# A gated scan in log levels: score levels with two heads per product, the projection's units spread anew, and decayed keys' exponents by eight ScalarE activations

## The reference, cut to what matters

```python
q = jax.nn.silu(q)
f = lbh + (1.0 - lbh) * jax.nn.sigmoid(fpre)
k = 1.0 - f
logf = jnp.log(f)
...
b = jnp.cumsum(lfc, axis=2)
inter = jnp.einsum('bhtd,bhde->bhte', qc * jnp.exp(b), S)
diff = b[:, :, :, None, :] - b[:, :, None, :, :]
decay = jnp.exp(jnp.where(mask, diff, -jnp.inf))
A = jnp.einsum('bhtsd,bhsd->bhts', qc[:, :, :, None, :] * decay, kc)
intra = jnp.einsum('bhts,bhse->bhte', A, vc)
b_last = b[:, :, -1:, :]
S_new = jnp.exp(b_last[:, :, 0, :])[..., None] * S + jnp.einsum(
    'bhsd,bhse->bhde', kc * jnp.exp(b_last - b), vc)
```

## Time and profile before

| | |
|---|---|
| median of 3 runs | 3231.85 us (3229.95 to 3232.8) |
| the profiled execution | 3230.88 us, its span 3229.1 us |
| TensorE busy | 2908.6 us, 90% of the span |
| TensorE's weight loads | 2611.5 us, 81% |
| VectorE busy | 1680.7 us, 52% |
| ScalarE busy | 687.4 us, 21% |
| GpSimd busy | 1098.1 us, 34% |
| mean granted clock of TensorE | 0.949 of full speed |

### The profile page before, as it was taken

How to read it: one execution, slowest core, us unless ns; L and a number is a source line. 1 busy time by engine, 2 the same in 40 slices (tenths; PEclk the granted TensorE clock), 3 DMA queues, 4 the chain that set the end, 5 groups by cost and what they waited for, 6 DMA issues and landing times.

```text
span 3229.1 us, 42488 instructions
## 1 busy us (share of the span) xinstructions
PE 2908.6 (90%) x18302; PEld 2611.5 (81%) x18302; DVE 1680.7 (52%) x2202; ACT 687.4 (21%) x1197; POOL 1098.1 (34%) x588
## 2 busy tenths in 40 slices
PE   6999777777998999899999988889999999899987
PEld 6887767777878987777777766779999999888887
DVE  3589667763512554444444467512365566455445
ACT  3111122223323410000000023211222222233421
POOL 7333131115632623322322225552322323212343
PEclk9999888878999999999999998999999999999998
DMA  5122321104311421111111124542332332355662
GB/s 195 63 85 98 93 85 53 43 30 149 125 66 67 157 79 52 48 44 40 40 52 40 40 91 150 173 153 79 118 92 89 108 118 93 117 183 185 226 223 92
DMA packets 148067, 325.62 MB, mean 101 GB/s; under 512 B 11148, under 2 KB 77608, under 8 KB 147752
## 3 DMA queue, kind: packets, MB, share of 16 engines
q10 hardware_dynamic: 105832, 169.80, 15.5%
q1 hardware_dynamic: 42048, 153.11, 14.7%
HBM read 245.26 MB, written 77.61 MB: 100 GB/s over the span
## 4 chain that ended last, share of the span: by engine, by line
PE 74%; DVE 13%; ACT 4%; DMA 2%; POOL 2%; issue 2%; ACTq 2%; DVEq 0%; POOLq 0%
PE pp L232 26%; PE pp L217 21%; PE pp L416 8%; PE pp L1698 7%; PE pp L2205 3%; POOL w_lo L2762 1%; PE pp L1608 1%; PE pp L1588 1%; DVE ffn_cb L572 1%; PE pp L1257 1%; DVE hgin_b L2034 1%; POOL w_hi L2760 1%; PE pp L369 1%; DMA ret_m<-m_s 1%; DMA w_raw<-in_weights 1%
## 5 line engine op out<-in xcount | busy, mean ns | idle before, releaser
L2760 POOL CAST w_hi<-w_raw 128x1024 fp32r<-128x1024 f32 x292 | 355.4, 1217 | 2082.0 <-PE pp L232 914.9
L232 PE MATMUL pp<-w_hi,act_hi 128*128 128x256 f32 x2688 | 780.6, 290 | 53.7 <-ACT hg_st L2074 24.7
L232 PE MATMUL pp<-w_lo,act_hi 128*128 128x256 f32 x2688 | 768.2, 286 | 0.0
L232 PE MATMUL pp<-w_hi,act_lo 128*128 128x256 f32 x2688 | 767.8, 286 | 0.0
L2762 POOL TENSOR_TENSOR w_lo<-w_raw,w_hi 128x1024 fp32r<-128x1024 f32 x292 | 750.6, 2571 | 23.4
L232 PEld LDWEIGHTS pp<-w_hi,act_hi 128*128 128x128 f32 x2688 | 523.9, 195 | 61.7 <-issue 24.9
L232 PEld LDWEIGHTS pp<-w_lo,act_hi 128*128 128x128 f32 x2688 | 523.9, 195 | 0.0
L232 PEld LDWEIGHTS pp<-w_hi,act_lo 128*128 128x128 f32 x2688 | 523.0, 195 | 0.0
L217 PE MATMUL pp<-act_hi,w_hi 128*128 128x512 f32 (+1 forms) x976 | 300.6, 389 | 1.6 <-POOL w_lo L2762 1.6
L217 PE MATMUL pp<-act_lo,w_hi 128*128 128x512 f32 (+1 forms) x976 | 300.6, 389 | 0.0
L217 PE MATMUL pp<-act_hi,w_lo 128*128 128x512 f32 (+1 forms) x976 | 300.4, 389 | 0.0
(11 more groups left out here) (398 smaller groups left out, 4331.5 us busy)
## 6 DMA issues: line engine op xcount, KB each, us to landing
w_raw<-in_weights SPq DMA_DIRECT2D x292, 512.0 KB, 3.8
z_s<-hg_st ACTq DMA_DIRECT2D x24, 1024.0 KB, 4.6
hg_qkb<-hT_s ACTq DMA_DIRECT2D x24, 512.0 KB, 6.4
qkvT_s<-mixin_o ACTq DMA_DIRECT2D x12, 512.0 KB, 2.9
gdn_qkv<-qkvT_s ACTq DMA_DIRECT2D x8, 768.0 KB, 5.3
front_x<-in_x ACTq DMA_DIRECT2D x8, 512.0 KB, 6.9
mix_x<-in_x ACTq DMA_DIRECT2D x8, 512.0 KB, 6.0
x_s<-mix_y ACTq DMA_DIRECT2D x8, 512.0 KB, 2.9
```

Of the source, the lines that this page charges most:

```text
L232: last = pe.matmul(dst, a[:, k, t * P:(t + 1) * P], w[slot][:, k * SC:k * SC + n], start=(k == 0 and a is high and w is w_hi), stop=(k == ...
L2760: pool.tensor_copy(hi, raw).then_inc(w_split, 1)
```

## The change

1. **Order in `hT_s`.** Heads are stored with the even ones first, then the odd ones; queries, keys and sums of the odd heads are written backwards in time (`kept`). The loads (`load`) bring each half apart: six DMAs for three, the odd half from the mirrored place. The values' columns are reordered in the weights on the host.
2. **Two heads per product.** With the odd heads reversed, the keys' halves of an even head and of its odd partner fill all 128 tokens, and so do the queries' halves. `KQ` holds four such pairs of keys and four of queries; one product per pair gives both heads' scores of the level, 4 products instead of 8. The masks are symmetric, `pick` copies 512 columns into `both`. After the levels, `join` writes the diagonal (L2362, L2363 of the changed kernel) and copies the upper triangle of `both` to the even heads and the lower, backwards, to the odd ones. `A` is no longer cleared. At level 0 the keys have no exponent: a copy (L2310) stands in its place, and ScalarE's exponent covers 512 columns.
3. **Values.** The odd heads' values are turned back in time by one product of 128 x 512 with a reversed identity (L2238) and a copy by ScalarE (L2183).
4. **Decayed keys.** The subtraction on VectorE goes; ScalarE makes exp(b_last - b) in eight activations (L2176), one per head, with a scale of -1 and the last sum as bias.
5. **Marks.** For t >= 1: 1, 3, 4, 6, 7, 9, 10, 10, 13, 13, 16. The output stands one unit behind the ninth of these, at 14. ScalarE's copies are given by the same marks (`m[l] - 3` before level l).
6. **Output store.** Two DMAs, even and odd heads, each in pieces of 128 columns.

The diff, cut to its core:

```diff
@@ HgInputs
+            def kept(self, x, j):
+                return backwards(x[:, :]) if j % 2 else x[:, :]
-                    self.qs.done(act.activation(self.q[j % 4][:, :], bank(2 * (j % 4)), ACT.Silu), "q")
+                    self.qs.done(act.activation(self.kept(self.q[j % 4], j), bank(2 * (j % 4)), ACT.Silu), "q")
-                    V.done(dve.tensor_scalar(self.k[s][:, :], f, -1.0, 1.0, ALU.mult, ALU.add), "k")
+                    V.done(dve.tensor_scalar(self.kept(self.k[s], j), f, -1.0, 1.0, ALU.mult, ALU.add), "k")
...
@@ Hgrn.marks
-                return [k + l for l in range(8)] + [k + 10, k + 11, k + 16]
+                return [k + l for l in (1, 3, 4, 6, 7, 9, 10, 10, 13, 13, 16)]
@@ Hgrn.act
-                        act.dma_start(self.qkb[s][:, j, :, :], hT_s[j].rearrange("(h p) n -> p h n", p=P)[:, :, t * P:(t + 1) * P]).then_inc(self.loaded[s], 16)
+                        for odd in range(2):
+                            at = t if odd == 0 else t // 4 * 4 + 3 - t % 4
+                            heads = slice(odd * HH // 2, (odd + 1) * HH // 2)
+                            act.dma_start(self.qkb[s][:, j, heads, :], hT_s[j].rearrange("(h p) n -> p h n", p=P)[:, heads, at * P:(at + 1) * P]).then_inc(self.loaded[s], 16)
-                            U.keep_to(act, m[0] - 3 + l)
+                            U.keep_to(act, m[l] - 3)
-                        after(act, V, "kdif", t)
-                        A.done(act.activation(self.E[0][:, :, :], self.E[0][:, :, :], ACT.Exp), "xk")
+                        b = self.qkb[t % 2][:, 2]
+                        for h in range(HH):
+                            end = P - 1 if h < HH // 2 else 0
+                            e = act.activation(self.E[0][:, h, :], b[:, h, :], ACT.Exp, scale=-1.0, bias=b[:, h, end:end + 1])
+                        A.done(e, "xk")
...
+                    after(act, PE, "jv", t)
+                    A.done(act.activation(self.v[t % 2][:, HH // 2:HH, :], bank(1).rearrange("p (h e) -> p h e", h=HH // 2), ACT.Copy), *(("xk", "kdr", "vr") if last else ("vr",)))
+                    U.keep_to(act, m[9] + 1)
                     after(act, PE, "o", t)
...
@@ Hgrn.pe
+                        if l < LEVELS:
+                            for j in range(HH // 2):
+                                last = pe.matmul(dst[:, j * P:(j + 1) * P], keys[:, j, :], keys[:, HH // 2 + j, :], start=True, stop=True)
+                        else:
+                            for h in range(HH):
+                                last = pe.matmul(dst[:, h * P:(h + 1) * P], self.qkb[s][:, 1, h, :], self.qkb[s][:, 0, h, :], start=True, stop=True)
...
+                    last = pe.matmul(bank(1), turn_back[:, :], self.v[s][:, HH // 2:HH, :].rearrange("p h e -> p (h e)"), start=True, stop=True)
+                    PE.done(last, *(("jv",) if t + 1 < NT else ("kdT", "jv")))
+                    U.make_to(pe, m[9] + 1)
+                    after(pe, A, "vr", t)
@@ Hgrn.dve
+                def of_queries(x, sz):
+                    return at_steps(x, sz, rows(sz), [HALF_ - sz, 2], [1, sz])
+                def as_queries(x, sz):
+                    return at_steps(x, HALF_ + sz, rows(sz), [-sz, 2], [1, sz])
-                    V.done(dve.memset(self.A[:, :, :], 0.0), "zero")
+                            if l:
+                                V.done(tt(as_keys(e, sz), mid, of_keys(b, sz), ALU.subtract), f"el{l}")
+                            V.done(tt(as_queries(e, sz), of_queries(b, sz), mid, ALU.subtract), f"er{l}")
...
+                V.done(dve.tensor_tensor(self.A[:, 0:n, :], raw[:, 0:n, :], unit, ALU.mult), "dg0")
+                V.done(dve.tensor_tensor(backwards(self.A[:, n:HH, :]), raw[:, n:HH, :], unit, ALU.mult), "dg1")
+                V.done(dve.copy_predicated(self.A[:, 0:n, :], self.mask(LEVELS), self.both[:, :, :]), "cpa")
+                V.done(dve.copy_predicated(backwards(self.A[:, n:HH, :]), self.mask(LEVELS + 1), self.both[:, :, :]), "cpb")
```

More of the change, by code:

```diff
@@ L203, in natural, with at_steps @@
             return x.rearrange("p h (b two n) -> p (h b) two n", two=2, n=1 << l)
+        def at_steps(x, first, *steps):
+            return bass.AP(x.tensor, x.offset + first, [list(x.ap[0]), *[list(a) for a in steps]])
         def weights_ready(pe, j):
@@ L2093, in __init__ @@
             def __init__(self, start):
[L2094 to L2099, removed]
+                dv = "er0"
+                for s in range(1, LEVELS + 2):
+                    dv += (f" el{s} er{s}" if s < LEVELS else "") + (f" klo{s - 1} kup{s - 1}" if s <= LEVELS else "") + (f" at{s - 2} cp{s - 2}" if s >= 2 else "")
+                dv += " dg0 dg1 ata cpa cpb qe0 qe kd ss " + recip_sqrt_steps("n") + " on " + " ".join(f"s{h}" for h in range(HH))
+                super().__init__("hg", pe=" ".join(f"a{l}" for l in range(LEVELS + 1)) + " kdT jv o ds",
+                                 act=" ".join(f"x{l}" for l in range(LEVELS)) + " xb xk kdr vr sq n_ln n_y", dve=dv, start=start)
                 b = self.buf
@@ L2138, in level @@
                 def level(t, l):
-                    after(act, V, f"eup{l}", t)
-                    A.done(act.activation(self.E[l % 2][:, :, :], self.E[l % 2][:, :, :], ACT.Exp), f"x{l}")
+                    after(act, V, f"er{l}", t)
+                    e = self.E[l % 2][:, :, :] if l else self.E[0][:, HH // 2:HH, :]
+                    A.done(act.activation(e, e, ACT.Exp), f"x{l}")
                 for t in range(NT):
@@ L2198, in pe @@
                             after(pe, V, f"kup{l}", t)
-                            lhs = rhs = self.KQ[l % 2]
-                        else:
-                            lhs, rhs = self.qkb[s][:, 1], self.qkb[s][:, 0]
                         if l >= 2:
                             after(pe, V, f"cp{l - 2}", t)
-                        for h in range(HH):
-                            last = pe.matmul(pp[l % 2][:, h * P:(h + 1) * P], lhs[:, h, :], rhs[:, h, :], start=True, stop=True)
+                        dst, keys = pp[l % 2], self.KQ[l % 2]
+                        if l < LEVELS:
[4 more added lines that the diff above has]
+                                last = pe.matmul(dst[:, h * P:(h + 1) * P], self.qkb[s][:, 1, h, :], self.qkb[s][:, 0, h, :], start=True, stop=True)
                         PE.done(last, f"a{l}")
@@ L2270, in dve, with queries @@
                             self.pick(dve, t, l)
-                    self.pick(dve, t, LEVELS)
+                    self.join(dve, t)
                     after(dve, A, "xb", t)
+                    def queries(*last):
+                        V.done(tt(self.KQ[1][:, 0:N, :], q[:, 0:N, :], self.E[1][:, 0:N, :], ALU.mult), "qe0")
+                        V.done(tt(backwards(self.KQ[1][:, N:HH, :]), q[:, N:HH, :], self.E[1][:, N:HH, :], ALU.mult), "qe", *last)
                     if t + 1 < NT:
-                        V.done(tt(self.KQ[1][:, :, :], q, self.E[1][:, :, :], ALU.mult), "qe")
-                        V.done(tt(self.E[0][:, :, :], b[:, :, P - 1:P].broadcast_to((P, HH, P)), b, ALU.subtract), "kdif")
+                        queries()
                         after(dve, A, "xk", t)
@@ L2844, in strips @@
             yield o.reshape(P, STRIP)
-    w_in, w_in2 = w["w_in"][0], w["w_in_2"][0]
+    w_in, w_in2 = w["w_in"][0], w["w_in_2"][0].copy()
+    values = w_in2[:, 2 * D:3 * D].reshape(D, HH // 2, 2, P)
+    w_in2[:, 2 * D:3 * D] = values.transpose(0, 2, 1, 3).reshape(D, D)
     qkv, gate, abl = w_in[:, 0:3 * GW], w_in[:, 3 * GW:4 * GW], w_in[:, 4 * GW:4 * GW + 2 * GH]
```

94 lines of the change are left out of this document (57 added, 37 removed).

## The result

The changed kernel takes 3243.5 us (median of 13 runs, 3239.4 to 3250.0), against 3231.9 for the one before: 1.0038 times as long, 95% interval 1.0030 to 1.0047. It is slower by 11.6 us. The prediction had 3222.6 us, 3206 to 3238, and gave "slower" 0.09. Its profiled execution took 3243.2 us at a span of 3241.3.

The account below looks back on a forecast made before the run. TensorE's own instructions were taken as the bound: -46.4 us saved, +34.0 for boundary waits with clock, +1.5 after tile 6, +0.6 after tile 0, +1.0 outside the scan, -9.3 in all from 3231.85: 3222.6 us, range 3206 to 3238.

Parts of the forecast that it names:

- TensorE's own work, -42.7 us: Scan: halved level products take 49.8 us off TensorE, turning the values back adds 7.1; net 42.7 us saved.
- Within a tile no wait: Inside a scan tile, VectorE's and ScalarE's steps all finish under TensorE's cover, so no wait was expected.
- The 2.6 us of copy waits: At tile ends, TensorE's waits for copies of projection units were all taken as gone, 2.6 us saved.
- The wait at the boundary: Between a tile's output and the next level 0, TensorE would wait 4.3 us; with clock, 34.0 us over five.
- a rival of 0.19: At boundaries, GpSimd's conversions hold the port during level 0 steps, adding 2.2 us to each wait: 3234.6 us; chance 0.19.
- The chain by ScalarE: At tile ends, store, loads, copy and strip's store put ScalarE's first exponent at O+12.0, O being the output products' end.
- Five boundaries: Full waits only after tiles 1 to 5; tile 0 keeps five units, after tile 6 about 1.5 us is left.
- The clock, 2.5 us a wait: After each 4.3 us boundary wait, TensorE runs at half the granted clock for a while, losing 2.5 us.
- Tile 0's keys, -1.1 us: In tile 0, the wait before the transposes, for the decayed keys, shrinks by 1.1 of its 1.3 us.
- Level 0's step pattern: VectorE's two level 0 steps hop between heads at every element: +0.38 us each, 2.05 us together.
- The prediction's second estimate: By the Trainium skill's figures for hopping elements, VectorE's two level 0 steps would be 0.7 us longer.
- Outside the scan, +1.0 us: In the stage before the scan, writing keys and sums backwards slows VectorE: 1.0 us, at most 2.1.

Follow-up runs that it names:

- e12: Changed kernel with every one of the seven levels' four products issued twice, same result: 3294.1 us.
- e13: Changed kernel with one more unit before level 0, tile 0's conversions three units later, loads in pairs behind level 2 to 4 exponents: 3185.5 us.
- e2: Changed kernel with ScalarE's loads of the tile after next issued behind the next tile's level 1 exponent, not before its level 0 exponent: 3249.8 us.
- e1: Changed kernel with GpSimd's conversions of the next weight strip let go by the strip's second unit, not its first: 3232.0 us.
- e5: Changed kernel with 48 extra unused products on TensorE ahead of the wait for level 0's product in tiles 2 to 7: 3233.4 us.
- e3: Changed kernel with both the edits of e1 and e2, conversions a unit later and loads later: 3212.0 us.
- e8: e1 with tile 0's conversions three units later, loads in three pairs behind level 2 to 4 exponents, values' load behind level 5: 3202.7 us.
- e11: e8 with the decayed keys' exponents again from two VectorE subtractions and one activation: 3206.8 us.
- e6: Changed kernel with the decayed keys' exponents again from two VectorE subtractions and one activation: 3256.9 us.
- e9: Changed kernel with one unit moved from ahead of the decayed keys to behind the state products, so four precede level 0: 3201.2 us.

## Why the prediction was wrong

- **TensorE's own work, -42.7 us: right.** e12 puts the levels' part at 50.6 for 49.8, and where no wait is left (e13) a tile is 6.2 us shorter; the sum has 5.3 by the work and 0.4 by the copy waits.
- **Within a tile no wait: right** in the changed kernel from tile 1 on. The 2.6 us of copy waits fell to 1.7.
- **The wait at the boundary, the failed step.** The prediction wrote "VectorE's two products follow at once", so GpSimd's hold of the port stood in the sum with nothing, and was a rival of 0.19, "against: a VectorE run without gaps also holds GpSimd off". The kernel before has rows for that argument, where four VectorE steps in a row keep a TENSOR_TENSOR of 2.4 us at 4.74:

```profile
2397.02 4.74 POOL L2762 TENSOR_TENSOR w_lo<-w_raw,w_hi 128x1024 fp32r<-128x1024 f32 x1
...
2397.03 0.67 DVE L2259 TENSOR_TENSOR hg_E<-hg_qkb 128x512 f32<-128x512 f32 x1
```

  But the earlier trace rows, from the same trace, show the opposite, in a run of VectorE without gaps too: steps of 1.53, 2.87, 1.52 and 2.87 us from 2164.40 on. The changed kernel has this second pattern at every boundary, and e2 has it with no gap anywhere. No conversion in the changed scan takes over 3 us. Which of the two patterns comes is not shown by any run. In place of "at once" the product of the queries stood for 2.92 us, and level 0 was ready at O+16.4 for the O+14.75 forecast: 6.08 us of wait instead of 4.3. The chain by ScalarE was right (O+12.3 for 12.0; 3.7 us of wait in e1 for 4.3) and was the second longest. That the rival's price came so near (6.5) is in part luck: it added 2.2 us to ScalarE's chain, while tile 6 and e2 show the same 6.1 us with the exponent 3.8 us sooner.
- **Five boundaries; there are six.** With the short loads ScalarE is early at the end of tile 6, GpSimd is not: 6.07 us where 1.5 was allowed. Together the two errors make 36.5 us of waits for 23.0.
- **The clock, 2.5 us a wait: 1.9** (e5), six times. (The row of 0.69 in the earlier trace rows puts the clock's return near 1232.6 and not 1232.3; it changes 0.1 us.)
- **Tile 0's keys, -1.1 us: wrong in sign,** +3.2 us of wait and some 2.4 of clock (transposes of 1.97 us for 0.87, and a unit of 4.15 us for 2.88 behind them). It is the same contention. I had allowed 2 us for it against a cover of 8.64; it held two steps for nearly 3 us each and a third for 1.55.
- **Level 0's step pattern: oversized.** Unblocked, the product takes 0.79 to 0.86 us (e1, e3, e8, e13) against 0.69 before; about +0.15, not +0.38, and the keys' step has become a copy of 0.51. The prediction's second estimate, 0.7 us for the two, was as far off, and the measured steps decide.
- **What I counted at nothing:** that the copies of units no longer stand behind VectorE's subtraction, worth 4 to 13 us by e11 and e6.
- **Outside the scan, +1.0 us: can't be told.** TensorE comes to the scan's first load 0.4 us later than before; kernels with the same code up to there come 2.5 us sooner (e9) to 1.6 later (e1).

Summed again with the measured terms: -42.7 + 36.5 (waits) + 11.4 (clock) + 5.6 (tile 0) - 0.9 (copies) + 1.2 (a longer first load, 11.9 us for 10.7) = +11.1. The spans differ by 12.2.

What stays open: why equal work behind the scan runs up to 7 us longer or shorter when it starts at another moment (e5, e2), and why VectorE's run holds GpSimd off at one place and takes turns with it at another. Not tried is the plain rival to the moves above: level 0's product ahead of level 1's arguments in VectorE's order.

## What to carry to other kernels

When work leaves the bounding engine, the order of what is left must be laid out anew from the slack between two points, counted in units on the engine that arrives and in microseconds on every chain that must be ready, and GpSimd's work, let go by TensorE's own position, is one of these chains. If two engines share a port, ask how many instructions of the one can fall ahead of the step that is waited for: each may hold it for its whole length, and a shift of one unit (2.9 us) can decide it, here for 42 us. After a change that saves work and gains nothing, look at which wait is new before undoing the change: here the idea was worth 50 us and three small moves brought them out.

## What the runs showed of the hardware

- Beside a GpSimd CAST or TENSOR_TENSOR of 128x1024, VectorE's 0.7 us steps on two SBUF inputs took 1.5 to 2.95 us; the held step ends 0.6 to 0.7 us behind GpSimd's. So did predicated copies with mask and data in SBUF (2.95 for 0.76). Those that read their data from the product memory were not held: 0.75 us beside a CAST and beside a TENSOR_TENSOR.
- In the changed scan GpSimd pays little: 2.39 us alone, up to 2.74 beside VectorE. In the kernel before its TENSOR_TENSOR took 4.6 to 4.75 us nine times in the scan, behind runs of VectorE.
- TensorE's granted clock was lower behind waits of 6.1 us at all six boundaries. Behind waits of 3.1 to 4.4 us in e1 it was so at some and not at others: level 0's eight instructions took 2.08 us behind 3.67 and 3.37, 1.16 behind 3.11, and 1.34 behind 4.00. With useless products in the wait it stayed at 2.4 GHz (e5, granted clock 1.00).
- Six DMA issues that carry three loads' bytes cost ScalarE 3.8 us instead of 3.2; behind an exponent, in a gap, they cost TensorE nothing.
